# First expert's rows by one-hot products from the rows in SBUF in place of a gather; cross-tile counts by three broadcast products

## The reference, cut to what matters

```python
h2 = rmsnorm(x2, norm_ffn)
coarse = softmax(h2 @ w_coarse)                      # 4 groups, the best one is taken
fine   = (h2 @ w_fine).reshape(512, 4, 4)[token, group]
top_w, expert_id = the two best of the group         # 2 of 16 experts for each token
gu  = h2 @ w_up[e]                                   # 1024 x 512
act = silu(gu[:, :256]) * gu[:, 256:] * gate
out = x2 + sum over experts of act @ w_down[e]       # 256 x 1024
```

## Time and profile before

| | us |
|---|---|
| median of 3 runs | 539.01 |
| lowest, highest | 538.91, 541.05 |
| profiled execution, its span | 539.0 |
| TensorE busy | 511.2 |
| VectorE, ScalarE, GpSimd busy | 394.0, 280.2, 176.5 |

### The profile page before, as it was taken

The page is one execution under the profiler, slowest core; times in us unless marked ns, Lnnn a source line. Parts: engine busy times, 40 slices in busy tenths (PEclk is TensorE's granted clock), DMA queues, the critical chain, the costliest instruction groups (busy, mean ns, idle before and its releaser), DMA issues.

```text
span 539.0 us, 7480 instructions
## 1 busy us (share of the span) xinstructions
PE 511.2 (95%) x2622; PEld 414.8 (77%) x2622; DVE 394.0 (73%) x658; ACT 280.2 (52%) x457; POOL 176.5 (33%) x348
## 2 busy tenths in 40 slices
PE   6999999999999999999999999779999999999992
PEld 3888877778778877878888888777887877777761
DVE  4889774997979979767558524568988878788740
ACT  5634144555655565643343212245767777877741
POOL 1229948689599000000000000032213232324344
PEclk9999999999999999999999999957999999999997
DMA  8560551122022101242587737579999999966433
GB/s 309 70 215 3 146 167 30 50 79 78 2 80 78 46 16 58 60 116 61 151 291 281 291 134 296 194 229 411 377 327 327 319 358 369 344 235 172 123 45 38
DMA packets 62775, 93.95 MB, mean 174 GB/s; under 512 B 14183, under 2 KB 45959, under 8 KB 62738
## 3 DMA queue, kind: packets, MB, share of 16 engines
q1 hardware_dynamic: 56304, 80.84, 43.9%
q0 software_dynamic: 5184, 8.41, 7.1%
q10 hardware_dynamic: 1250, 4.22, 2.0%
HBM read 88.19 MB, written 12.58 MB: 187 GB/s over the span
## 4 chain that ended last, share of the span: by engine, by line
PE 76%; DVE 7%; POOL 5%; SPq 4%; DMA 3%; issue 2%; ACT 2%; POOLq 0%; DVEq 0%; ACTq 0%
PE pj L1730 10%; PE pj L1732 9%; PE pj L1731 9%; PE pj L2103 6%; PE pj L2104 5%; PE pj L2105 5%; PE m L2124 5%; PE tp L2089 3%; SPq L511 2%; PE m L2129 1%; PE m L2131 1%; PE m L2130 1%; PE pj L1847 1%; PE m L1730 1%; PE sc L1822 1%
## 5 line engine op out<-in xcount | busy, mean ns | idle before, releaser
L1730 PE MATMUL pj<-h_high,split 128*128 128x512 f32 x192 | 76.6, 399 | 0.2 <-DVE h_low L1422 0.2
L1732 PE MATMUL pj<-h_high,split 128*128 128x512 f32 x192 | 74.9, 390 | 0.0
L1731 PE MATMUL pj<-h_low,split 128*128 128x512 f32 x192 | 74.8, 390 | 0.0
L612 POOL TENSOR_TENSOR rstd<-ssq,half_col 128x1 f32<-128x1 f32 x8 | 4.4, 556 | 184.7 <-DVE ssq L1094 171.1
L1603 DVE TENSOR_TENSOR up_low<-arena_front,up_high 128x2048 fp32r<-128x2048 f32 x23 | 52.7, 2292 | 11.2 <-ACT up_high L971 11.2
L2103 PE MATMUL pj<-up_high,xt_high 128*128 128x512 f32 x128 | 51.4, 402 | 0.9 <-DVE xt_low L1637 0.9
L2104 PE MATMUL pj<-up_low,xt_high 128*128 128x512 f32 x128 | 51.0, 398 | 0.0
L2105 PE MATMUL pj<-up_high,xt_low 128*128 128x512 f32 x128 | 50.8, 397 | 0.0
L971 ACT ACTIVATE up_high<-arena_front 128x2048 fp32r<-128x2048 f32 x23 | 44.2, 1928 | 10.8 <-PE pj L2105 9.7
L712 POOL DMA_INDIRECT out_dram<-arena_back,idx_all x12 | 23.6, 1964 | 64.4 <-DMA out_dram<-arena_back,idx_all 46.7
L412 ACT ACTIVATE split<-arena_front 128x2048 fp32r<-128x2048 f32 (+1 forms) x20 | 34.7, 1739 | 18.4 <-PE sc L1732 10.9
(11 more groups left out here) (348 smaller groups left out, 1324.6 us busy)
## 6 DMA issues: line engine op xcount, KB each, us to landing
arena_front<-in_w_expert_up_dram SPq DMA_DIRECT2D x23, 1024.0 KB, 12.2
arena_back<-in_w_expert_down_dram SPq DMA_DIRECT2D x16, 1024.0 KB, 13.0
arena_front<-in_w_in_dram SPq DMA_DIRECT2D x12, 1024.0 KB, 5.6
arena_back<-in_w_expert_up_dram SPq DMA_DIRECT2D x9, 1024.0 KB, 13.5
arena_front<-in_w_out_dram SPq DMA_DIRECT2D x4, 1024.0 KB, 5.0
arena_back<-in_x_dram SPq DMA_DIRECT2D x4, 512.0 KB, 6.4
arena_front<-in_w_ssm_glu_gate_dram SPq DMA_DIRECT2D x8, 256.0 KB, 2.9
arena_front<-in_w_ssm_glu_val_dram SPq DMA_DIRECT2D x8, 256.0 KB, 3.5
```

The costliest lines, as they stand in the source:

```text
L1730: pe.matmul(dst, sh, mh, start=first and i == 0, stop=False)
L1731: pe.matmul(dst, sh, ml, start=False, stop=False)
L1732: ins = pe.matmul(dst, sl, mh, start=False, stop=last and i == len(terms) - 1)
```

## The change

Expert 0's rows are no longer gathered and transposed. For its list, VectorE writes four tiles of one-hots with the row's 1/rms in place of the 1 (`first_pick`, plain float32), and TensorE multiplies each chunk of 128 columns of `x2` (as stationary operand) with them, summed over the four tiles: 8 x 4 products that leave the transposed, picked rows in the banks `tp`. ScalarE and VectorE split each chunk and multiply it with the norm's gain, which is loaded once more in the order of `row_chunk` (`gain_run`). List 1 is placed ahead of this block and list 0 behind it; the gather of expert 1 is the first one. Lists 2 and 3 are placed behind the sixth chunk of expert 0's products. ScalarE splits expert 1's first weight half ahead of the chunks. The waits of SP, GpSimd and the counts of `xt_full` and its kin move accordingly. The six cross-tile count products become three, whose moving operand is one tile's flags repeated for all later tiles. The diff, less some of its unchanged lines:

```diff
@@ -197,6 +197,8 @@
         gain_col = sb("gain_col", [P, DC])
+        gain_run = sb("gain_run", [P, DC])
+        first_pick = part("att", 1280 + 2 * D, TT * CAP, t=TT, n=CAP)
@@ -299,6 +301,7 @@
         first_idx, shares_done = sem("first_idx"), sem("shares_done")
+        first_picked, first_rows, first_high, first_low = (sem(n) for n in ("first_picked", "first_rows", "first_high", "first_low"))
@@ -465,6 +468,10 @@
+        def first_bank(k):
...
+            return tp[k // 4][:, (k % 4) * P:(k % 4 + 1) * P]
@@ -517,6 +524,8 @@
             sp.dma_start(gain_col[:], norm_ffn[0].rearrange("(k p) -> p k", p=P)).then_inc(small_loaded, 16)
+            sp.dma_start(gain_run[:].rearrange("p (a b) -> p a b", b=2),
+                         norm_ffn[0].rearrange("(a p b) -> p a b", p=P, b=2)).then_inc(small_loaded, 16)
@@ -558,10 +567,11 @@
             load_half(6)
-            sp.wait_ge(gathered[0], 16)
+            sp.wait_ge(gathered[1], 16)
...
             sp.wait_ge(x2_stored, 16 * TT)
+            sp.wait_ge(first_rows, DC)
@@ -683,8 +693,8 @@
-                if e >= 2:
-                    g.wait_ge(xt_full, 2 * (e - 1))
+                if e >= 3:
+                    g.wait_ge(xt_full, 2 * (e - 2))
@@ -720,11 +730,12 @@
                     add_rows(e - 5)
-                if e < 2:
-                    g.wait_ge(first_idx, e + 1)
-                elif e in LISTS:
+                if e == 1:
+                    g.wait_ge(first_idx, 1)
+                elif e and e in LISTS:
                     g.wait_ge(idx_done, LISTS.index(e) + 1)
-                gather(e)
+                if e:
+                    gather(e)
@@ -973,9 +984,17 @@
                 for f in range(2):
-                    act.wait_ge(xt_full, e * 2 + (f + 1))
+                    act.wait_ge(xt_full, (e - 1) * 2 + (f + 1))
...
+            def high_first_rows():
...
+                act.wait_ge(small_loaded, 16 * 16)
+                for k in range(DC):
+                    if k % 4 == 0:
+                        act.wait_ge(first_rows, k + 4)
+                    act.activation(xt_high[:, k, :], first_bank(k), ACT.Copy, scale=gain_run[:, k:k + 1]).then_inc(first_high, 1)
@@ -1006,7 +1025,7 @@
             def step(e):
-                if e + 1 < NE:
+                if 0 < e < NE - 1:
@@ -1029,7 +1048,8 @@
             act.activation(below, below, ACT.Exp).then_inc(r_act, 1)
-            high_rows(0)
+            high_up(1, 0)
+            high_first_rows()
@@ -1190,7 +1210,7 @@
             v.wait_ge(const_ready, 4)
-            v.wait_ge(small_loaded, 16 * 15)
+            v.wait_ge(small_loaded, 16 * 16)
@@ -1602,11 +1622,21 @@
-            for e in range(2):
-                pick_list(e)
-            for e in range(2):
-                v.wait_ge(idx_full, e + 1)
-                ts(idx_all[:, e:e + 1], sc[e][:, 128:129], float(SEQ), None, ALU.add).then_inc(first_idx, 1)
+            def low_first_rows(ks):
...
+                for k in ks:
+                    if k % 4 == 0:
+                        v.wait_ge(first_high, k + 4)
+                    stt(xt_low[:, k, :], first_bank(k), gain_run[:, k:k + 1], xt_high[:, k, :].bitcast(F32), ALU.mult, ALU.subtract
+                        ).then_inc(first_low, 1)
...
+            pick_list(1)
+            for t in range(TT):
+                ts(first_pick[:, t, :], slot_no[:], pos[:, 0, t:t + 1], rstd[:, TT + t:TT + t + 1], ALU.is_equal, ALU.mult
+                   ).then_inc(first_picked, 1)
+            pick_list(0)
+            v.wait_ge(idx_full, 1)
+            ts(idx_all[:, 1:2], sc[1][:, 128:129], float(SEQ), None, ALU.add).then_inc(first_idx, 1)
@@ -1621,9 +1651,13 @@
             low_up(0, 0)
+            low_first_rows(range(DC // 2))
+            low_up(0, 1)
+            low_first_rows(range(DC // 2, DC))
...
             v.wait_ge(idx_full, 3)
+            ts(idx_all[:, 0:1], sc[0][:, 128:129], float(SEQ), None, ALU.add)
@@ -1632,7 +1666,7 @@
                 for f in range(2):
-                    v.wait_ge(xt_high_done, e * 2 + (f + 1))
+                    v.wait_ge(xt_high_done, (e - 1) * 2 + (f + 1))
@@ -1652,9 +1686,7 @@
-            low_rows(0)
             read_lists(1)
-            low_up(0, 1)
@@ -2038,9 +2070,10 @@
             pe.matmul(sc[0][:, 0:TT * NE], before[:], chosen[:].rearrange("p t e -> p (t e)"), start=True, stop=False)
-            for t in range(TT):
-                for later in range(t + 1, TT):
-                    ins = pe.matmul(sc[0][:, later * NE:(later + 1) * NE], ones[:], chosen[:, t, :], start=False, stop=t == TT - 2)
+            for t in range(TT - 1):
+                later = TT - 1 - t
+                ins = pe.matmul(sc[0][:, (t + 1) * NE:TT * NE].rearrange("p (t e) -> p t e", t=later), ones[:],
+                                chosen[:, t:t + 1, :].broadcast_to([P, later, NE]), start=False, stop=t == TT - 2)
@@ -2050,7 +2083,7 @@
-                pe.wait_ge(pick_done, e + 1)
+                pe.wait_ge(pick_done, 2 - e)
@@ -2080,11 +2113,21 @@
+            def pick_first_rows():
...
+                pe.wait_ge(first_picked, TT)
+                for k in range(DC):
+                    for t in range(TT):
+                        ins = pe.matmul(first_bank(k), row_chunk(x2[:, t, :], k), first_pick[:, t, :], start=t == 0, stop=t == TT - 1)
+                    ins.then_inc(first_rows, 1)
...
             def turn_rows(e):
-                pe.wait_ge(gathered[e % 2], 16 * (e // 2 + 1))
+                pe.wait_ge(gathered[e % 2], 16 * ((e + 1) // 2))
                 for f in range(2):
-                    if e:
-                        pe.wait_ge(xt_done, e * 2 + (f - 1))
+                    if e == 1:
+                        pe.wait_ge(first_low, DC // 2 * (f + 1))
+                    else:
+                        pe.wait_ge(xt_done, (e - 1) * 2 + (f - 1))
@@ -2093,8 +2136,10 @@
                 for k in ks:
-                    if k % (DC // 2) == 0:
-                        pe.wait_ge(xt_done, e * 2 + 1 + k // (DC // 2))
+                    if e == 0:
+                        pe.wait_ge(first_low, k + 1)
+                    elif k % (DC // 2) == 0:
+                        pe.wait_ge(xt_done, (e - 1) * 2 + 1 + k // (DC // 2))
@@ -2142,14 +2187,18 @@
-            for e in range(2):
-                place_index(e)
+            place_index(1)
+            pick_first_rows()
+            place_index(0)
             place_shares()
-            turn_rows(0)
-            pe.wait_ge(idx_done, 1)
-            place_lists(LISTS[1], LISTS[2])
             for e in range(NE - 1):
-                up(e, range(DC))
+                if e == 0:
+                    up(e, range(DC - 2))
+                    pe.wait_ge(idx_done, 1)
+                    place_lists(LISTS[1], LISTS[2])
+                    up(e, range(DC - 2, DC))
+                else:
+                    up(e, range(DC))
...
                     place_lists(LISTS[e + 2], LISTS[e + 3])

```

## The result

| | before | changed |
|---|---|---|
| median, us | 539.94 (4 runs, 538.91 to 541.05) | 544.47 (4 runs, 543.57 to 545.18) |
| ratio, 95% interval | | 1.0082, 1.0056 to 1.0108 |
| profiled execution: time, span | not listed, 539.0 | 545.04, 543.0 |

The change makes the kernel **slower by 0.8%**, some 4.4 us (544.47 against 539.94 is 4.5, the ratio 1.0082 gives 4.4). The 539.94 is the median with a fourth run of the kernel before, 540.87, beside the three that gave 539.01. The forecast was 541.1 and no change; the first rival, a clock that falls in the new wait, had said 543.1.

What follows compares the result with a forecast made beforehand. TensorE, busy 95% of the span, was taken as the bound, with expert 1's start as the mark. From 539.0 us, +0.5 for an added load issue and +1.6 for expert 1's later start gave 541.1 us, range 536.8 to 544.3.

Steps and rivals of the forecast that it cites:

- the first rival: At expert 1's start, the clock falls while TensorE waits, some 4 us low costing 2.0: 543.1 us, chance 0.33.
- the new wait: Ahead of expert 1, late lists 2 and 3 hold VectorE's queue; TensorE waits 3.4 us, expert 1 starts 1.6 later.
- 64 records: Expert 0's 32 one-hot products leave two records each, at 0.22 us low clock and 0.115 high; block ends at 363.9.
- two microseconds or more: Sign that the forecast is right: a VectorE wait this long, ending with the placing of lists 2 and 3.
- The counts: In the routing, three count products in place of six save VectorE's wait 0.7 us.
- the two pauses of the earlier trace: TensorE pauses at 346.0 to 349.2 and 530.2 to 533.5, each followed by the low clock.
- point of decision: At expert 1's start, the clock's fall was taken to be decided from a pause near 3.3 us.
- the base: Starting time of the sum: the profiled execution's 539.0 us, taken as the median of three runs, 539.01, without correction.
- The clock came back: In expert 0's one-hot block, the high clock was to return 6.1 us after 353.6, with 27.7 records low.
- The start: In SP's queue, one more small load ahead of the second weight piece was to cost +0.5 us.
- The clock does not return during the block: Rival: expert 0's one-hot block runs all at the low clock, ending 3.8 us later: 544.9 us, chance 0.08.
- The removed wait wins: Rival: block ends at 360.7 to 362.2 and expert 1 may start 3.5 to 5 us early: middle 537.0, chance 0.16.

Runs made afterwards that it cites:

- experiment 11: Changed kernel, expert 1's first VectorE weight split ahead of its list wait, `gain_run` loaded later, unread products filling TensorE's pauses; the last experiment: 536.51 us, ratio 0.9937.
- experiment 4: Changed kernel with lists 2 and 3 placed behind expert 0's fourth chunk instead of its sixth: 542.05 us, ratio 1.0032.
- experiment 7: Changed kernel with VectorE's first weight split of expert 1 ahead of its list wait and `gain_run` loaded behind the fifth weight piece: 540.76 us, ratio 1.0004.
- experiment 9: Kernel before, with products that nobody reads filling TensorE's pauses around the routing and in the last expert: 538.01 us, ratio 0.9959.
- experiment 3: Changed kernel with 14 products that nobody reads in TensorE's pause ahead of expert 1: 542.16 us, ratio 1.0033.
- experiment 6: Kernel before with only the `gain_run` load added on SP ahead of the second weight piece, its rows unused: 540.15 us, ratio 1.0007.
- experiment 5: Changed kernel with `gain_run` loaded behind the fifth weight piece, with its own semaphore: 543.86 us, ratio 1.0061.
- experiment 2: Changed kernel with VectorE's first weight split of expert 1 ahead of its wait for lists 2 and 3: 540.71 us, ratio 1.0005.

## Why the prediction was wrong

**What held.** The path is the one written down. The block has 64 records: in the last experiment (359.42 - 351.86) / 64 = 0.118 us each at the high clock, predicted 0.115. The Trainium skill (TensorE: Matmul & The Clock Gate, Back-to-back issue gap) with its 81 ns would have had it too fast; the measurement decides. VectorE waits 2.33 us for lists 2 and 3 ("two microseconds or more"), its queue behind that takes 376.51 - 370.02 = 6.5 us, as worked out, and TensorE waits 3.15 for 3.4. The gathers of experts 1 and 2 are hidden. The counts give their 0.7 as far as `pos`.

**The step that failed: the clock in the new pause.** The sum priced the new wait by its length alone, +1.6 us, took expert 1 at the high clock, and put the fall of the clock at nothing; as a rival the fall had 0.33 against 0.42. The clock fell in the wait, and the experts behind it took 2.7 us longer. The pause was named as the place, and the two pauses of the earlier trace rows with little or no work in them that were followed by the low clock spoke for the fall; the pause of 1.4 us without one was no match for mine of 3.4. The rows favoured the rival, and the chances should have been the other way. The rival's point of decision, a pause near 3.3 us, does not hold either: the clock fell behind waits of 1.80, 0.95 and 0.93 us (experiments 4, 7 and 9). The Trainium skill (TensorE: Matmul & The Clock Gate, What's actually happening) has the low clock as the resting state that activity lifts; this trace agrees, the clock falling in the pause at 375.54 and coming back at 382.36, behind 5.85 us of dense work, and so does experiment 3, where activity alone keeps it. The rival's price was low too: 2.0 us from some 4 us at the low clock; it was 5.85 us, hence 2.9, or 2.7 by the marks.

**The second step: the base.** "Whose time, 539.0 us, is the median of the three runs, 539.01; nothing needs correcting" took the span for the time. In the executions listed with both the time exceeds the span by 1.7 to 2.2 us (545.04 and 543.0 above; 541.41 and 539.4 in one of the kernel before). A span of 539.0 thus belongs, by estimate, to an execution of about 541, the highest of the three (541.05). Its own sum starts there: 541 + 2.1 = 543.1, and 2.7 for the clock makes 545.8; the profiled execution of the changed kernel took 545.04. The median of 539.01 was low by itself, too: it is 539.94 with the fourth run. From there 539.9 + 2.1 + 2.7 = 544.7, and 544.47 was measured. Of the 3.4 us by which the forecast was missed, the clock is thus 2.7 and the base 0.9; the rest is the terms below, which nearly cancel, and that is luck.

**Sizes that were off.** The clock came back 4.5 us into the block, not 6.1: the block took 9.57 us, not 10.3 (9.0 to 10.2 in the other profiles without fillers ahead of it). Expert 1's start at 376.51 looks like the predicted 376.6, but the first count product came 0.7 later than before, so the stage itself was 0.8 shorter than predicted: 0.7 in the block, and 0.35 ahead of `pos`, where the clock was still high; the small products behind the block took a little more. Against the kernel before's profile it is 0.9 longer, not 1.6; against that of experiment 6 it is 1.9. The start lost 0.7, not 0.5; experiments 5 and 6 cannot tell what of it is the load. A low-clock product of 512 columns was priced 0.447; the rows have 0.43 from start to start (377.10 to 377.53).

**Rivals.** "The clock does not return during the block" fell: it did. "The removed wait wins" fell as well: it wanted the clock back within 3 us of the block's start, and it took 4.5, and VectorE's queue held expert 1 as forecast. With that queue mended (experiments 2 and 7) the time is level with before, within 0.25% either way by their intervals. Only with the clock held up (experiment 11) is a kernel with the block faster than the kernel before, and there the fillers have a part in it.

**What stays open.** Why experiment 7, whose TensorE reaches expert 1 sooner by 0.4 to 1.5 us, is not faster over twelve runs is shown by its one profile only. The executions of one kernel spread by 3 to 5 us. In the kernel before most of that goes with the clock: of the 78 executions timed beside the experiments, the 22 with a mean granted clock of 0.972 to 0.974 took 541.5 us (median), the 55 with 0.976 or more 539.3. What decides which executions lose the clock in a short pause was not found. The rest, the start's issue times and the end behind the last product (8.0 to 9.2 us, 10.8 in experiment 6), was not taken apart.

## What to carry to other kernels

When a product group is moved to a later place on TensorE, look at the engine that reads its result: everything queued behind that read moves too, here 6.5 us of VectorE for two small lists. Price a new TensorE wait twice, by its length and by the clock behind it; here the second was the larger, 2.7 us of the 4.0 between the spans. Where one profile gives a stage 24.5 us, a second of the same TensorE program may give 23.4, so a gain under a microsecond wants several profiles or a like clock on both sides. And a gain from removing a wait shows in the time only if no other pause near it lets the clock fall; products that nobody reads, put into the pauses, are a cheap test of that and here a gain of their own, 0.4% on the kernel before (ratio 0.9959) and 0.7% on the mended one (1.0004 to 0.9937).

## What was not expected of the hardware

- The clock fell around a wait of 1.80 us and, in other kernels, of 0.95 and 0.93 us, where list products of 4 columns and transposes stood just ahead (experiments 4, 7 and 9). In experiment 2 the same 0.95 us, behind the same small products, passed at 1.00. So neither a wait's length nor what stands ahead of it tells by itself.
- TensorE can be busy by its records and stay at the low clock: the kernel before stood at 0.50 from 353.4 to 369.5 with 12.94 of 16.1 us busy. Up to 363.57 these are small products and transposes, 7.0 of 10.2 us busy, and then 5.9 us of dense ones. In experiment 11, with nine products of 512 columns ahead of the count products and three ahead of list 1, the clock was 1.00 from 340 to 500.
- One issue in SP's queue at the start is long, and it moves: 1.94 us for `gain_run` in the changed kernel's profile and 0.58 in four others, where in three of them a router load beside it took 1.50 to 1.57. The two loads of `b_re` took 6.7 to 8.3 us.
